# A transformer kernel's expert stage: seventeen first load slots, the first quad taken through its down projection before the later gathers, and zero products around the router and in the last quad

## The reference

```
x = x + mixed @ w_out
hf = rmsnorm(x, ffn_norm)
g_sel = argmax(hf @ w_rg + b_rg)             # one of 4 groups
e_in  = (hf @ w_re + b_re)[group g_sel]      # 8 experts in it
top_vals, top_idx = top_k(e_in, 2)
weight = softmax(g_logits)[g_sel] * softmax(top_vals)
y[t] = sum over the 2 experts e of
       weight[t, e] * (silu(h[t] @ w_g[e]) * (h[t] @ w_u[e])) @ w_d[e]
out = rmsnorm(x + y, final_norm)
```

## Time and profile before

| what | us |
|---|---|
| median of 3 runs | 1584.33 |
| lowest, highest | 1580.31, 1586.98 |
| the profiled execution, its own time | 1581.68 |
| span of its trace | 1579.8 |
| PE busy | 1440.3 (91%) |
| DVE busy | 898.3 (57%) |
| ACT busy | 617.9 (39%) |
| DMA queue of the loads, share of 16 engines | 67.3% |

### The profile page before, as it was taken

How to read it: one execution, slowest core, us unless ns; L and a number is a source line. 1 busy time by engine, 2 the same in 40 slices (tenths; PEclk the granted TensorE clock), 3 DMA queues, 4 the chain that set the end, 5 groups by cost and what they waited for, 6 DMA issues and landing times.

```text
span 1579.8 us, 26709 instructions
## 1 busy us (share of the span) xinstructions
PE 1440.3 (91%) x11441; PEld 1284.5 (81%) x11441; DVE 898.3 (57%) x1041; ACT 617.9 (39%) x736; POOL 19.2 (1%) x24
## 2 busy tenths in 40 slices
PE   4999999999999999999998999999989997965565
PEld 2899998889999999999998999999878896722323
DVE  2787775658777778778665555565555453100001
ACT  2544345545434454434433444444345533200001
POOL 0000000400000000000000000000000000000000
PEclk8999999999999999999998999999999997978878
DMA  9998767337978579875653556545343375599996
GB/s 341 301 328 305 277 241 238 108 117 260 326 282 292 202 271 329 306 277 192 195 182 104 183 182 187 184 143 173 101 134 107 107 269 218 233 421 421 421 420 247
DMA packets 203333, 380.31 MB, mean 241 GB/s; under 512 B 12661, under 2 KB 157946, under 8 KB 190970
## 3 DMA queue, kind: packets, MB, share of 16 engines
q1 hardware_dynamic: 203258, 379.22, 67.3%
HBM read 378.14 MB, written 1.05 MB: 240 GB/s over the span
## 4 chain that ended last, share of the span: by engine, by line
PE 79%; DMA 11%; DVE 5%; ACT 3%; issue 1%; SPq 1%; DVEq 0%; ACTq 0%
PE ps L635 17%; PE ps L637 16%; PE ps L636 16%; PE ps L663 10%; DMA plain_wlo<-in_w_exp_up_dram 9%; PE ps L664 5%; PE ps L1338 3%; ACT whi L1464 2%; PE ps L1323 2%; DVE wlo L1875 2%; DMA ada_raw<-in_w_ada_dram 2%; PE ps L750 1%; PE ps L991 1%; PE ps L803 1%; DMA raw<-in_ffn_wd_dram 1%
## 5 line engine op out<-in xcount | busy, mean ns | idle before, releaser
L1875 DVE TENSOR_TENSOR wlo<-raw,whi 128x2048 fp32r<-128x2048 f32 (+1 forms) x188 | 425.4, 2263 | 248.0 <-ACT whi L1464 247.9
L1464 ACT ACTIVATE whi<-raw 128x2048 fp32r<-128x2048 f32 (+1 forms) x188 | 354.6, 1886 | 172.9 <-PE ps L637 143.2
L635 PE MATMUL ps<-h_both,whi 128*128 128x256 f32 x1320 | 380.4, 288 | 1.1 <-DVE wlo L1875 0.9
L637 PE MATMUL ps<-h_both,wlo 128*128 128x256 f32 x1320 | 373.9, 283 | 0.0
L636 PE MATMUL ps<-h_both,whi 128*128 128x256 f32 x1320 | 373.9, 283 | 0.0
L635 PEld LDWEIGHTS ps<-h_both,whi 128*128 128x128 f32 x1320 | 251.7, 191 | 10.2 <-issue 5.2
L663 PE MATMUL ps<-h_both,whi 128*128 128x512 f32 x704 | 253.7, 403 | 2.5 <-DVE h_both L1885 2.5
L636 PEld LDWEIGHTS ps<-h_both,whi 128*128 128x128 f32 x1320 | 251.9, 191 | 0.8 <-issue 0.5
L637 PEld LDWEIGHTS ps<-h_both,wlo 128*128 128x128 f32 x1320 | 251.9, 191 | 0.0
L635 PE MATMUL ps<-hidhi,whi 128*128 128x256 f32 x704 | 201.2, 286 | 2.1 <-DVE wlo L2012 2.1
L637 PE MATMUL ps<-hidhi,wlo 128*128 128x256 f32 x704 | 199.3, 283 | 0.0
(11 more groups left out here) (301 smaller groups left out, 1849.6 us busy)
## 6 DMA issues: line engine op xcount, KB each, us to landing
ada_raw<-in_w_ada_dram SPq DMA_DIRECT2D x72, 1024.0 KB, 5.4
raw<-in_ffn_wg_dram SPq DMA_DIRECT2D x44, 1024.0 KB, 6.5
raw<-in_ffn_wu_dram SPq DMA_DIRECT2D x44, 1024.0 KB, 5.4
raw<-in_ffn_wd_dram SPq DMA_DIRECT2D x44, 1024.0 KB, 6.8
raw<-in_w_in_dram SPq DMA_DIRECT2D x18, 1024.0 KB, 5.3
ada_raw<-in_w_exp_gate_dram SPq DMA_DIRECT2D x16, 1024.0 KB, 19.9
raw<-in_w_exp_up_dram SPq DMA_DIRECT2D x16, 1024.0 KB, 16.8
plain_whi<-in_w_exp_down_dram SPq DMA_DIRECT2D x16, 1024.0 KB, 16.8
```

What stands on the lines that cost most here:

```text
L635: pe.matmul(o, wh, xh, start=start, stop=False, skip_group_check=shared)
L637: return pe.matmul(o, wl, xh, start=False, stop=stop, skip_group_check=shared)
L1464: act.activation(whi[s][:, 0:width], raw[s][:, 0:width], ACT.Copy).then_inc(high[s], 1)
L1875: dve.tensor_tensor(wlo[s][:, 0:width], raw[s][:, 0:width], whi[s][:, 0:width].bitcast(F32), ALU.subtract).then_inc(split[s], 1)
```

## The change

**Load slots.** Tiles for weights are now given per quad: `first_w`, `second_w` for quads 0 and 1, `later_w` for the rest, picked by `expert_w(q, kind, j)`. To make room, `htok_hi` and `htok_lo` move from the arena to `mhi` and `mlo`, and `h_slots` becomes four separate areas. Seventeen loads now come ahead of the first that waits for an expert product: all twelve of quad 0, the four gate loads of quad 1 and its first up load. The first two are issued after `o_split` 8, ahead of unit 31. Quad 1's other seven wait for quad 0's products, kind by kind. The last quad's down matrices are loaded in two halves each (row k = 0 of all four, then k = 1), with semaphores of their own for the second halves.

**Order on PE.** 44 zero products stand ahead of the ranks and 8 behind them. The gather runs all products with `htok_hi` first, then those with `htok_lo`. GATE of quad 0 waits for `h_slots` piece by piece. The order is then: gather 0, GATE 0, UP 0, slot weights, turn 0, down 0, `pickT`, GATE 1, UP 1, gathers 1 to 3, scatter 0, turn 1, down 1, scatter 1, and from there each quad in full. In the last quad 44 zero products stand between GATE and UP, the 30 ahead of the down projection are gone, and its k = 0 products come first, then 22 zero products, then k = 1.

**DVE and ACT.** The low parts of the second token half come after the first `pick`; the rest of `pick` comes after the first gather is copied. Both engines do quad 0's outputs and quad 1's hidden values ahead of the later gathers' copies.

```diff
-            sp.wait_ge(sem("mixed"), 1)
-            expert_load(GATE, 0, 0)
+            sp.wait_ge(sem("o_split"), 8)
+            expert_load(0, GATE, 0)
+            expert_load(0, GATE, 1)
+            load_unit("blk2", 31)
+            expert_load(0, GATE, 2)
+            expert_load(0, GATE, 3)
+            sp.wait_ge(split[2], n_loads[2])
+            expert_load(0, UP, 0)
             sp.wait_ge(sem("mixed"), 2)
...
+            expert_load(0, UP, 1)
+            expert_load(0, UP, 2)
+            sp.wait_ge(sem("mixed_split"), 2)
+            expert_load(0, UP, 3)
             sp.wait_ge(split[0], n_loads[0])
-            expert_load(UP, 0, 0)
+            expert_load(0, DOWN, 0)
...
             sp.wait_ge(used[0], n_loads[0])
-            expert_load(DOWN, 0, 0)
-            expert_load(DOWN, 1, 1)
+            expert_load(1, GATE, 0)
+            expert_load(1, GATE, 1)
             sp.wait_ge(used[1], n_loads[1])
...
+            expert_load(1, GATE, 2)
+            expert_load(1, GATE, 3)
+            expert_load(1, UP, 0)
+            sp.wait_ge(expert_used[GATE], 1)
+            expert_load(1, UP, 1)
+            sp.wait_ge(expert_used[UP], 1)
+            expert_load(1, UP, 2)
+            expert_load(1, UP, 3)
+            expert_load(1, DOWN, 0)
+            sp.wait_ge(expert_used[DOWN], 1)
+            for j in range(1, 4):
+                expert_load(1, DOWN, j)
+            for q in range(2, NQ):
                 for kind in (GATE, UP, DOWN):
                     sp.wait_ge(expert_used[kind], q)
-                    for j in range(4):
-                        expert_load(kind, j, 4 * q + j)
+                    for row in ((0, 1) if kind == DOWN and q == NQ - 1 else (None,)):
+                        for j in range(4):
+                            expert_load(q, kind, j, row=row)
...
+            zeros_into(ps[:, 2, 0:T], 44)
             wait("router_sel")
...
+                for part in (htok_hi, htok_lo):
+                    if r == 0:
+                        wait("htok_high" if part is htok_hi else "htok_split", 4)
...
+                    if q == 0 and kind == GATE and k % 2 == 0:
+                        pe.wait_ge(sem(("gathered_act", "gathered_dve")[k // 2 % 2]), k // 4 + 1)
...
+                    if last and first == (0, 0):
+                        zeros_into(ps[:, GATE, 0:T], 22)
...
+            zeros_into(ps[:, 2, 0:T], 8)
             wait("picked")
-            wait("htok_split", 4)
             gather(0, slice(0, T))
...
             into_hidden(0, GATE)
+            wait("ranks_read")
+            into_hidden(0, UP)
...
-            into_hidden(0, UP)
-            for r in range(1, 4):
-                gather(r, slice(r * T, (r + 1) * T))
...
+            hidden_turn(0)
+            out_of_hidden(0)
...
+            into_hidden(1, GATE)
+            into_hidden(1, UP)
+            for r in range(1, 4):
+                gather(r, slice(r * T, (r + 1) * T))
...
+            scatter(0)
+            for q in range(1, NQ):
+                if q > 1:
                     into_hidden(q, GATE)
+                    if q == NQ - 1:
+                        zeros_into(ps[:, 7, 0:T], 44)
                     into_hidden(q, UP)
                 hidden_turn(q)
-                if q == NQ - 1:
-                    zeros_into(ps[:, GATE, 0:T], 30)
                 out_of_hidden(q)
                 scatter(q)
```

More of the change, by code:

```diff
@@ L317, in build @@
         expert_landed = [[sem(f"{kind}_landed{j}") for j in range(4)] for kind in ("gate", "up", "down")]
+        last_row_landed = [sem(f"last_row_landed{j}") for j in range(4)]
         expert_used = [sem(f"{kind}_used") for kind in ("gate", "up", "down")]
@@ L525, in _, with expert_load @@
             dense("ffn3", 1, 1, None)
-            for u in range(32):
+            for u in range(31):
                 load_unit("blk2", u)
-            def expert_load(kind, j, e):
+            def expert_load(q, kind, j, e=None, row=None):
+                e = 4 * q + j if e is None else e
                 w = (a["w_exp_gate_2"], a["w_exp_up_2"], a["w_exp_down_2"])[kind]
@@ L1349, in out_of_hidden @@
             def out_of_hidden(q):
-                for j in range(4):
-                    pe.wait_ge(expert_landed[DOWN][j], 16 * (q + 1))
                 pe.wait_ge(sem("moe_hidT"), q + 1)
@@ L1355, in out_of_hidden @@
                     pe.wait_ge(sem("y_split"), 2 * q)
-                for n in range(2):
-                    for k in range(2):
+                last = q == NQ - 1
+                for first, second in (((0, 0), (0, 1)), ((1, 0), (1, 1))) if last else (((0, 0), (1, 0)), ((0, 1), (1, 1))):
+                    for k, n in (first, second):
+                        if (k, n) == (0, 0) or last and n == 0:
+                            for j in range(4):
+                                if k:
+                                    pe.wait_ge(last_row_landed[j], 16)
+                                else:
+                                    pe.wait_ge(expert_landed[DOWN][j], 16 * (q + 1))
                         for j in range(4):
                             sl = slice(SLOTS * j, SLOTS * (j + 1))
-                            mm = pe.matmul(ps[sl, 6 + n, :], hidT[:, k, sl], expert_w[DOWN][j][:, k * D + n * 512:k * D + (n + 1) * 512],
-                                           start=(k == 0), stop=(k == 1))
-                    if n == 0:
-                        mm.then_inc(sem("y_half"), 1)
+                            mm = pe.matmul(ps[sl, 6 + n, :], hidT[:, k, sl], expert_w(q, DOWN, j)[:, k * D + n * 512:k * D + (n + 1) * 512],
+                                           start=(k == 0), stop=(k == 1), skip_group_check=True)
+                        if (k, n) == (1, 0):
+                            mm.then_inc(sem("y_half"), 1)
+                    if last and first == (0, 0):
+                        zeros_into(ps[:, GATE, 0:T], 22)
                 mm.then_inc(expert_used[DOWN], 1)
@@ L1773, in _ @@
             wait("token_rs")
-            for half in range(2):
-                for t in range(2):
+            for t in range(2):
+                for half in range(2):
                     copy(by_block(token_half(htok_hi, t, half)), turned(t, half), rs[:, t:t + 1]).then_inc(sem("htok_high"), 1)
-            refill(1)
             wait("logits_ready")
@@ L1793, in gathered_high @@
                     for k in (2 * i, 2 * i + 1):
[L1794 removed]
+                        ins = copy(h_slots[to][:, k, :], ps[:, 2 + i, (k % 2) * T:(k % 2 + 1) * T], gdeal[:, k:k + 1])
                     ins.then_inc(sem("gathered_act"), 1)
@@ L1820, in _ @@
             expert_silu(0)
-            for r in range(1, 4):
-                gathered_high(r, r)
+            hidden_out(0)
+            output_high(0)
             for i in range(NQ // 2):
@@ L1825, in _ @@
                 copy(pickT[:, 2 * i:2 * i + 2, :], ps[:, 6 + i % 2, :].rearrange("p (q t) -> p q t", q=2)).then_inc(sem("pickT_ready"), 1)
-            for q in range(NQ):
-                if q:
+            expert_silu(1)
+            for r in range(1, 4):
+                gathered_high(r, r)
+            for q in range(1, NQ):
+                if q > 1:
                     expert_silu(q)
@@ L2401, in _ @@
             for half in range(2):
-                for t in range(2):
-                    htok_low(t, half)
+                htok_low(0, half)
             wait("ranked")
@@ L2474, in _ @@
             expert_hidden(0)
+            link(dve.tensor_tensor(spill, weight, spill, ALU.mult))
+            output_low(0)
+            expert_hidden(1)
             for r in range(1, 4):
                 gathered_low(r, r)
-            link(dve.tensor_tensor(spill, weight, spill, ALU.mult))
-            for q in range(NQ):
-                if q:
-                    expert_hidden(q)
+            output_low(1)
+            for q in range(2, NQ):
+                expert_hidden(q)
                 output_low(q)
```

116 lines of the change are left out of this document (58 added, 58 removed).

## The result

| | median us | lowest to highest | profiled execution |
|---|---|---|---|
| before, 5 runs on this chip | 1584.33 | 1580.31 to 1586.98 | 1581.68 (span 1579.8) |
| changed, 5 runs | 1569.38 | 1563.92 to 1571.46 | 1569.38 (span 1567.5) |

The ratio is 0.9904, with a 95% interval of 0.9877 to 0.993. Forecast were 1567, with a range of 1560 to 1576: 17.4 us less by the forecast, 15.0 by the medians.

What follows compares the result with a forecast made beforehand. The prediction took the expert loads on the DMA queue as the limit. It summed 14.2 us at the last load and 3.2 us behind it to 17.4 us off the 1584.3 median: 1567 us, range 1560 to 1576.

Steps and rivals of the forecast that it cites:

- Part 1, the slots: Expert load queue: seventeen early loads instead of twelve, four of the five more filling the first hole; gain 12.5 us.
- fourth rival: Early loads don't fill the first hole: 12.5 us lost, 1579.5, no measurable change; chance 0.05.
- part 4: Loads beside the chain: one 14 us hole until 1386.6, then 64 loads at 2.503 us; last load 14.2 us earlier.
- Part 2, the router: Zeros put the ranks at full clock; gather 0 starts 1.2 us earlier, at 1316.5, and GATE 0 follows without a stop.
- Part 3, the chain on PE: PE steps that free slots, GATE 0 to down 1: down 0 6.4 us, ending 1343.9; down 1 ends 1385.5.
- first rival: Down 0 keeps the full clock: 2.7 us less, 1564; chance 0.20.
- second rival: PE is cold in two more steps of the chain, 2.7 us each: 1572; chance 0.20.
- Part 5, the tail: Behind the last load: UP 7 at full clock, down matrices in halves with zeros between; 3.2 us saved.
- more than 8 us from the last up landing to the last load's: Sign of being wrong, in the last quad's loads; the forecast had 7.4 us between them.
- The sum: Whole kernel: -14.2 at the last load and -3.2 behind it, -17.4 us in all, median 1567.

Runs made afterwards that it cites:

- x1: The changed kernel with quad 1's five early loads waiting for GATE 0's product, so twelve loads run ahead instead of seventeen; ratio to before 0.9901.
- x2: The changed kernel with quad 0's first five loads waiting until the second mixer is done, the seventeen places kept; ratio to before 0.99.
- x3: The changed kernel without the router's 44 and 8 zero products; ratio to before 0.9901.
- x6: The changed kernel with the last quad as before: whole down loads, no zeros around UP 7, 30 zeros ahead of down 7; ratio to before 0.9906.
- x7b: The changed kernel with the old PE order, gathers 1 to 3 and the picks' turns ahead of down 0, sixteen first places; ratio to before 0.9952.
- x9: The changed kernel with the edits of x5 and x11 together: interleaved order, thirty slot-weight products between GATE 1 and UP 1; ratio to before 0.9819.
- x8: The changed kernel with zero products added among the slot weights, ahead of quad 0's turn and ahead of down 0; ratio to before 0.9887.
- x11: The changed kernel with thirty of thirty-two slot-weight products moved from ahead of down 0 to between GATE 1 and UP 1; ratio to before 0.9879.
- x5: The changed kernel with down 1 ahead of gather 1, and GATE 2 and UP 2 behind gathers 1 and 2; median 1555.23 us, ratio to before 0.9815.

## Why the prediction was right, and where its steps were off

The times of its steps, on the clock face of before (the changed kernel's minus 4.14):

| step | forecast | measured |
|---|---|---|
| gather 0 starts | 1316.5 | 1316.6 |
| GATE 0 ends | 1328.1 | 1328.2 |
| down 0 ends | 1343.9 (1341.2 at full clock) | 1343.3 |
| gathers 1 to 3 end | 1377.6 | 1377.2 |
| down 1 ends | 1385.5 | 1386.3 |
| end of the span | 1562.4 | 1563.4 |

- **Part 1, the slots: right as to what happens, wrong as to its worth.** The first hole was filled and the queue full to 1317 (1321 on its own face). But the gain of 12.5 us of load time and the fourth rival's 1579.5, for early loads that don't fill the hole, were mis-sized: x1 and x2 put 1.5 and 0.0 us on it. The prediction's own part 4 held the reason, a hole of 14 us behind these loads, and the rival wasn't checked against it. Had SP been stuck, the kernel would still have been some 15 us faster than before.
- **Part 2, the router: the times right, the credit partly wrong.** Zeros bring 1 us at gather 0; that GATE 0 follows without a stop, at the full clock, doesn't hang on them (x3), and what it does hang on is argued, not shown.
- **Part 3, the chain on PE: right, in part by luck.** Down 0's end fits to 0.6 us because two errors cancel: the slot weights took 4.28 us instead of 3.67, down 0 5.28 instead of 6.4. Down 0 was forecast at 6.4 us and its first rival at 3.7; in the twelve kernels that have it right behind UP 0's hidden values it took 3.68 to 6.46 us, 5.28 in the changed one. Neither was "the" answer: the moment at which the clock falls differs from run to run. Down 1 was 0.8 us late, because scatter 0 took 3.3 us instead of the 1.9 forecast; the second rival's cold step fell on the scatter, not on a projection.
- **Part 4, the loads: right.** One hole of 14 us (14.7 measured) and then none. The 64 loads took from 1391.5 to about 1552.5, 2.516 us each instead of 2.503: 0.8 us more. (The end of the last load is read from windows in which the DMA share sinks over two microseconds, so this 0.8, and the 0.6 below, are good to about half a microsecond.)
- **Part 5, the tail: -3.2 forecast, -2.5 to -2.9 by x6**, all of it UP 7's clock. The zeros ended at 1544.17, half a microsecond after the loads would have let UP 7 start: in the runs of x1 to x3, where the loads released it, restart to end is 176.7 to 176.9 instead of 177.1. The halves brought nothing of the difference. One of the prediction's own signs of being wrong was set wrong: "more than 8 us from the last up landing to the last load's" came true (1543.3 to 1553.5, 10.2 us), and so it does in the kernel before (1553.7 to 1563.5, 9.8 us). Its 7.4 us had set a landing against the end of a window, 1561.0.
- **The sum.** From 17.4 to 16.4: 0.8 us at down 1, 0.8 in the price of the loads, less 0.6 at the end (15.0 us behind the last load instead of 15.6).

The 16.4 us themselves: GATE 0 ends 3.9 us earlier behind the mixer (1 of it from the zeros, 2.8 from GATE 0 without its stop and at the full clock), and from GATE 0 on 12.5 us are saved (247.7 to 235.2), which x7b ties to the order (11.9) and x6 to UP 7 (2.5). These two make more than 12.5, as x7b, which has the new tail, takes 0.6 us less than before from GATE 0 on and not 2.5: its down 0 comes 0.8 us later behind GATE 0, and 1.1 us stay unexplained.

## What to carry to other kernels

In these runs a queue that runs dry several times has one hole that counts, the last: loads that run early ahead of it are lost in it, and work of the releasing engine that is taken out ahead of the restart comes out at the end, unless the clock takes it back on the way (x9). So count the loads left at the last restart and the work of the releasing engine up to it, and cost every early transfer against the hole behind it. When that hole is closed, the one before it becomes the last and the same early loads get their price back (1.5 us, then 8.1). Long work that frees nothing (23.4 us of gathers) belongs in pieces between the short products that free places.

## What the runs showed of the hardware

- Gather products (weights strided in the tile, 128x256) take 0.25 us at a granted clock of 0.50 and 0.24 at 1.00; the clock even rose to full meanwhile (x3: 0.50, then 0.74, and GATE 0 at 1.00). The cold engine cost gather 0 nothing (7.98 us against 7.99).
- The clock fell to 0.50 with TensorE busy without a pause (x8, 3.10 of 3.10 us), behind a stretch of four-column products. With the same instructions ahead of it, down 0 took 3.68 us in one run and 5.35 in another (x9 and x11), so the zeros that should guard such a place can't be priced by one profile.
- Even the unchanged second mixer differs so: from its last low part to the router's second turn it is 51.5 us in eight of the fourteen kernels and up to 54.1 in the others (x5, where the clock was at 0.50 for the first 6 us). This is why distances were taken from GATE 0.
- 1 MB loads in a full queue ran at 407 to 421 GB/s in the long windows above. The Trainium skill, "DMA: Bandwidth & Descriptors", section "Bandwidth", gives 341 GB/s for a transfer of 1 MB and 425 GB/s for one of 16 MB, both issued from GpSimd. The queued 1 MB loads here, issued from SyncE, ran like the larger one. The 0.5 MB halves at the end landed no later than whole loads in x6, and 1.3 us later in x8.
